# A streaming-encoder block whose front runs in five segments: the segments' sizes, when they run, and which engine adds which rows

## The reference, cut to what matters

```python
q = (h @ w_q).reshape(Bb, S, PEER_HEADS, 2, PEER_HALF)          # 8 heads, two halves of 128
scores = jnp.einsum('bshpd,pnd->bshpn', q, sub_keys)             # 128 keys for each half
vals, idx = lax.top_k(scores, 16)
cand = vals[..., 0, :, None] + vals[..., 1, None, :]             # 16 x 16 sums
top_vals, pos = lax.top_k(cand, 16)                              # 16 of 16384 experts
gates = softmax(top_vals)
u = jnp.take(u_tab, e, axis=0)                                   # 1024 numbers for each expert
act = gelu(jnp.einsum('td,thkd->thk', xt, u))
vv = jnp.take(v_tab, e, axis=0)
y = jnp.einsum('thk,thkd->td', g * act, vv)                      # added to x
```

## Time and profile before

| | us |
|---|---|
| median of 3 runs | 3558.37 (3557.22 to 3565.75) |
| the profiled execution, its own time | 3558.73 |
| its span, first to last instruction | 3556.9 |
| TensorE matmul busy | 2871.3 (81%) |
| VectorE busy | 2532.2 (71%) |
| ScalarE busy | 1419.6 (40%) |
| GpSimd busy | 1284.6 (36%) |
| moved by DMA | 1376.58 MB, mean 387 GB/s |

### The profile page before, as it was taken

How to read it: one execution, slowest core, us unless ns; L and a number is a source line. 1 busy time by engine, 2 the same in 40 slices (tenths; PEclk the granted TensorE clock), 3 DMA queues, 4 the chain that set the end, 5 groups by cost and what they waited for, 6 DMA issues and landing times.

```text
span 3556.9 us, 35414 instructions
## 1 busy us (share of the span) xinstructions
PE 2871.3 (81%) x11192; PEld 1930.2 (54%) x11192; DVE 2532.2 (71%) x5329; ACT 1419.6 (40%) x3606; POOL 1284.6 (36%) x1028
## 2 busy tenths in 40 slices
PE   8878978899878787686998889778878687686765
PEld 7767856776544455363665557454445355363323
DVE  0248877767888887699678876798566756677664
ACT  2333453324344443334344453434343443433522
POOL 0014332323454444344434433433334333344441
PEclk9989989999989899888999899889999899898987
DMA  6589988989999999999999999999999999999995
GB/s 237 172 320 421 377 315 327 365 331 384 421 422 415 404 421 421 420 392 404 422 421 420 405 383 412 416 413 395 422 421 421 421 410 421 420 417 412 421 421 218
DMA packets 195916, 1376.58 MB, mean 387 GB/s; under 512 B 22401, under 2 KB 24321, under 8 KB 32018
## 3 DMA queue, kind: packets, MB, share of 16 engines
q0 software_dynamic: 147456, 1073.81, 73.5%
q1 hardware_dynamic: 48274, 300.51, 21.4%
HBM read 1363.22 MB, written 11.01 MB: 386 GB/s over the span
## 4 chain that ended last, share of the span: by engine, by line
PE 34%; DMA 30%; DVE 18%; issue 9%; ACT 7%; POOL 2%; another core or an unknown queue 0%; DVEq 0%; POOLq 0%; ACTq 0%; SPq 0%
DMA uv<-in_uv,idx 29%; PE bank L588 13%; PE ysum L780 8%; PE bank L598 8%; DVE acc L1321 5%; DVE uv L1293 4%; POOL uv L545 2%; PE bank L657 2%; DVE lidx L1146 1%; DVE vals L1143 1%; ACT bufX L856 1%; DMA slab<-in_slabs 1%; DVE bufE L1140 1%; DVE bufX L1111 1%; ACT bufX L813 1%
## 5 line engine op out<-in xcount | busy, mean ns | idle before, releaser
L545 POOL DMA_INDIRECT uv<-in_uv,idx x1024 | 1284.4, 1254 | 2214.9 <-DVE acc L1321 1033.5
L1293 DVE SCALAR_TENSOR_TENSOR uv<-uv,hbuf 128x1024 f32<-128x1024 f32 x1024 | 1247.2, 1223 | 550.8 <-DMA uv<-in_uv,idx 526.4
L780 PE MATMUL ysum<-uv,diag 128*128 128x512 f32 x2152 | 1121.3, 665 | 418.7 <-ACT diag L1044 416.4
L780 PEld LDWEIGHTS ysum<-uv,diag 128*128 128x128 f32 x2152 | 433.6, 211 | 965.9 <-ACT diag L1044 514.1
L1321 DVE SCALAR_TENSOR_TENSOR acc<-uv,dots,acc 128x1024 f32<-128x1024 f32 x486 | 622.3, 1281 | 86.6 <-ACT dots L1035 69.9
L1030 ACT ACTIVATE dots<-dots 128x2 f32<-128x2 f32 x512 | 103.0, 201 | 1148.3 <-DVE uv L1293 1137.0
L588 PE MATMUL bank<-bufA,slab 128*128 128x256 f32 (+1 forms) x2400 | 439.3, 342 | 5.5 <-ACT bufB L813 5.4
L588 PEld LDWEIGHTS bank<-bufA,slab 128*128 128x128 f32 x2400 | 390.8, 194 | 74.1 <-issue 36.4
L598 PE MATMUL bank<-slab,bufA 128*128 128x256 f32 x1408 | 318.1, 385 | 4.9 <-ACT bufA L842 3.7
L598 PEld LDWEIGHTS bank<-slab,bufA 128*128 128x128 f32 x1408 | 271.3, 194 | 63.5 <-issue 20.8
L1035 ACT ACTIVATE dots<-dots,gexp 128x1 f32<-128x1 f32 x1024 | 245.9, 287 | 20.9 <-ACT dots L1030 0.4
(11 more groups left out here) (146 smaller groups left out, 2426.5 us busy)
## 6 DMA issues: line engine op xcount, KB each, us to landing
slab<-in_slabs SPq DMA_DIRECT2D x255, 1024.0 KB
uv<-in_uv,idx POOLq DMA_INDIRECT x1024
x_d<-acc SPq DMA_DIRECT2D x7, 512.0 KB, 8.1
bufA<-in_x SPq DMA_DIRECT2D x3, 1024.0 KB
bufA<-x_d SPq DMA_DIRECT2D x3, 1024.0 KB
out<-bufA SPq DMA_DIRECT2D x3, 1024.0 KB
bufE<-in_g_ffn SPq DMA_DIRECT2D x5, 512.0 KB, 9.0
bufX<-in_g_fin SPq DMA_DIRECT2D x5, 512.0 KB, 20.9
```

The source lines that it names most:

```text
L545: nc.gpsimd.indirect_dma_start(out=uv[:, at % NS, :], out_offset=None, in_=a["uv"], in_offset=bass.IndirectOffsetOnAxis(ap=idx[:, g % 4, k ...
L780: ins = mm(ysum[:, c, :], diag[:, m % DS, :], uv[:, at % NS, D + c * 512:D + c * 512 + 512], start=(m == first), stop=(m == last))
L1293: v.scalar_tensor_tensor(out=row, in0=row, scalar=1.0, in1=hbuf[:, i % HB, :], op0=ALU.mult, op1=ALU.mult, accum_out=dots[:, g % 3, k:k + ...
```

## The change

The segments become 1, 1, 2, 2 and 2 tiles, so `AT` goes from (0, 1, 3, 5, 7) to (0, 1, 2, 4, 6) and `MOVED` from tiles 2, 4, 6 to 3, 5, 7. The second segment, now one tile, is due in step 28 instead of 50, and the closing of segment 0 with its opening puts two stages in a step. The due steps of the other segments follow from the same rule as before: 114, 242 and 370. Only groups 0 and 1 have their tails in a segment now (3 and 4); the tail of tiles 4 and 5 stands by itself, from step 405. The lists of a tile go by the tile's number modulo 3 instead of its place in the segment. Tiles 0 and 1 give 5 of a head's 16 rows to TensorE (`SOME`), tiles 2 to 5 `ODD`, tiles 6 and 7 `MOST`, from a tile's row 6 on.

```diff
@@ -1,3 +1,4 @@
+import math
 from contextlib import ExitStack
 
 import numpy as np
@@ -30,7 +31,7 @@
 LOW = -3.0e38
 
 
-SEGS = (1, 2, 2, 2, 1)
+SEGS = (1, 1, 2, 2, 2)
 NSEG = len(SEGS)
 TT = max(SEGS)
 SEG = TT * P
@@ -45,6 +46,8 @@
 
 NS = 10
 HB = 2
+
+LS = 3
 STEPS = TOPK // 2
 ROWS = NHEAD * TOPK
 END = NHEAD * STEPS
@@ -56,11 +59,12 @@
 
 
 ODD = tuple(range(1, TOPK, 2))
+SOME = tuple(range(1, TOPK, 3))
 MOST = tuple(k for k in range(TOPK) if k % 4)
-ON_PE = [MOST, ODD, ODD, ODD, ODD, MOST, MOST, MOST]
-
-SPARE = [100] + [6] * (NTILE - 1)
-IS_PE = [at % TOPK in ON_PE[at // (NH * TOPK)] and at % (NH * TOPK) >= SPARE[at // (NH * TOPK)] and at < ROWS - 4
+ON_PE = [SOME, SOME, ODD, ODD, ODD, ODD, MOST, MOST]
+
+SPARE = 6
+IS_PE = [at % TOPK in ON_PE[at // (NH * TOPK)] and at % (NH * TOPK) >= SPARE and at < ROWS - 4
          for at in range(ROWS)]
 
 PE_UPTO, DVE_UPTO = [0], [0]
@@ -71,7 +75,7 @@
 
 
 GROUPS = ((0, 1), (2, 3), (4, 5), (6,), (7,))
-HOST = {0: 2, 1: 3, 2: 4}
+HOST = {0: 3, 1: 4}
 GUEST = {h: q for q, h in HOST.items()}
 TAIL = ["T0", "T1", "pg0", "pg1", "pg2", "pg3", "pp", "mx", "T2"]
 LAST_GROUP = len(GROUPS) - 1
@@ -129,6 +133,11 @@
 BEHIND.update({f"lg{b + 1}": f"va{b}" for b in range(2 * TT - 1)})
 
 
+
+
+DUE = [AT_ONCE - 2, PER_TILE // 2 - 4] + [PER_TILE * AT[s] - AHEAD - 2 for s in range(2, NSEG)]
+
+
 def plan():
 
     found = []
@@ -142,14 +151,14 @@
         names = front_names(s)
         if not s or s - 1 in GUEST:
             names = OPENING + names
-        due = PER_TILE * AT[s] - AHEAD - 2 if s else AT_ONCE - 2
+        due = DUE[s]
         last = len(names) - 1
         begin = found[-1][0] + 1 if found else due - last
         for i, n in enumerate(names):
             stand(s, n, begin + i * (due - begin) // last)
-        more, gap = closing(s), 2 if s in GUEST else 1
-        for i, (of, n) in enumerate(more):
-            stand(of, n, due + gap * (i + 1))
+        pace = 2 if s in GUEST else 1 if s else 0.5
+        for i, (of, n) in enumerate(closing(s)):
+            stand(of, n, due + math.ceil(pace * (i + 1)))
     for q, tiles in enumerate(GROUPS):
         if q == LAST_GROUP:
 
@@ -339,8 +348,8 @@
         acc = sb("acc", [P, 2, D])
         x2 = [acc[:, (NTILE - 1) % 2:(NTILE - 1) % 2 + 1, :] if q == LAST_GROUP else x1 for q in range(len(GROUPS))]
         diag = sb("diag", [P, DS, P])
-        vals = sb("vals", [P, TT, NH, 2, TOPK])
-        lidx = sb("lidx", [P, TT, NH, 2, TOPK], U32)
+        vals = sb("vals", [P, LS, NH, 2, TOPK])
+        lidx = sb("lidx", [P, LS, NH, 2, TOPK], U32)
         lidf = sb("lidf", [P, 2, TOPK])
         tv = sb("tv", [P, TOPK])
         negmax = sb("negmax", [P, 1])
@@ -1132,7 +1141,8 @@
                 lists = []
                 for t in range(SEGS[s]):
                     for half in range(2):
-                        lists.append((vals[:, t, h, half, :], lidx[:, t, h, half, :],
+                        slot = (AT[s] + t) % LS
+                        lists.append((vals[:, slot, h, half, :], lidx[:, slot, h, half, :],
                                       ysc[:, h % 2, t, half * NK:half * NK + NK]))
                 for c in (slice(0, 8), slice(8, 16)):
                     if c.start:
@@ -1220,7 +1230,7 @@
 
                 base = TK * m
                 i, h = divmod(m, NH)
-                slot = i - AT[seg_of(i)]
+                slot = i % LS
                 val = vals[:, slot, h]
                 if base + j:
                     dve.wait_ge(topk_step, base + j)
```

## The result

The changed kernel takes 3535.55 us (median of 6 runs, 3530.7 to 3545.11) against 3559.94 for the kernel before (6 runs): ratio 0.993, 95% interval 0.9914 to 0.9946, that is 24 us or 0.7% faster.

The account below looks back on a forecast made before the run. DMA bytes at 421.5 GB/s were taken as the bound: 3266 us, plus starved time (DMA engines short of work) of 113 at start-up, 111 in the steps and 43 at the end, gave 3533 of span, so 3534; range 3498 to 3575.

Parts of the forecast that it names:

- three demands of about equal size: Steps 15 to 50 before: DMA 260 us, PE 267, DVE 242, taking turns and stretching each other to 320.
- C: Steps 50 to 114, segment 2's two-tile front: DMA 400 us, PE 356, DVE 350; 22 us starved.
- The transfers of patterns: Steps 136 to 242 repeat 72 to 178 of before, 13 us starved; 242 to 370 repeat 178 to 306, 26.
- A: Steps -7 to 28, two stages in a step beside rows: 28 us starved, with bounds of 8 and 65.
- the ring: Gather slots, 10 rows holding 25 us; expected to cover the lone tail of tiles 4 and 5, steps 405 to 421.
- 417 GB/s or more: Sign: from step 370 the windows read at least this rate until the last 80 us.
- The milestones: Signs: step 50 at about 690 us, step 306 at some 2300, in front only from about step 430.
- Behind at both: Sign: later than the kernel before at step 50 (690 against 666.3 us) and step 306 (2300 against 2268.7).
- The crowd did not dissolve: Rival, 13%: the evener work up to step 136 starves little, 63 us in all over the plan's steps; 3485 us.
- only passed on: Rival, 20%: steps -7 to 28 and 50 to 114 starve 78 us, not 50; 3562 us, no change.
- lockstep: Rival, 12%: in steps 5 to 27 chained stages wait behind row work, 12.4 us a step; 3617 us, half covered 3575.
- The clock rival: Rival, 5%: PE's low clock makes late steps without stages take 6.5 us against 4.98, costing 90 us; 3624 us.

Follow-up runs that it names:

- e1: Changed kernel with the second segment due in step 50 again and one stage a step in the first closing: 3567.2 us, ratio to before 1.0016.
- e2: Changed kernel with the old split of the rows between TensorE and VectorE: 3567.2 us, ratio to before 1.0011.
- e4: Changed kernel with the stages of the lone tails three steps apart instead of two: 3527.2 us, ratio to before 0.9904.
- e5: Changed kernel loading only half the columns of each weight piece after the first three: 3433.5 us, ratio to before 0.9645.
- e6: Kernel before, loading only half the columns of each weight piece after the first three: 3435.9 us, ratio 0.9648.
- e3: Kernel before with the new split of the rows alone: 3578.9 us, ratio 1.0054.
- e8: Changed kernel with the second segment due in step 36 instead of 28: 3536.1 us, ratio to before 0.993.
- e9: e4 with segment 2's closing, with segment 3's opening, at 1.75 steps a stage instead of 1: 3522.6 us, ratio to before 0.9895.
- e10: e9 with segment 4's closing and the tail inside it at 2.5 steps a stage instead of 2: 3519.8 us, ratio to before 0.9888.

## Why the prediction was right

The forecast was 3534 us with 3515 to 3549 for the likeliest case; measured are 3535.6, and a span of 3533.1 against 3533 in the sum.

*The bound.* The account, bytes at a ceiling of 421.5 GB/s plus starved time, gave the right sum. But it can't be tested by the total: with the same bytes, a difference in span is a difference in starved time by definition. What the runs test is where it arises, and there the placing of the crowds is shown: taking back the run-ahead brings 59 us into steps 72 to 114 (e1), the old split 32 into 306 to 370 (e2), and the tail's pace works on steps 405 to 421 (e4). e5 and e6 add how thin the bound is, and correct the picture that I had of steps 15 to 50: of "three demands of about equal size" that stretch each other, the weight bytes are none, for half of them can go and the stretch stays at 320 us (e6). Nor do VectorE's late additions set it (e3).

*The terms.* C was right in each part: 168.6 MB forecast, 426.2 x 0.397 = 169.2 moved; PE 356 and 353.8 us; DVE 350 and 351.0; starved 22 and 24.8. Steps 114 to 136: PE 149 and 147.4, starved 15 and 13.1. The transfers of patterns held: 136 to 242 has 9.7 (13) and 242 to 370 has 31.6 (26; the same stages starve 23 to 28 in e1, e4, e8, e9 and e10), in the places in which steps 72 to 306 had them. Steps 114 to 370 took 1602.8 us, and steps 50 to 306 of before 1602.4.

*Two terms failed, in opposite directions.* A was priced at 28 us for want of a row with two stages in a step, and took 14.4 (16 to 21 in later runs with the same plan there): DMA share 1.01 up to step 15 with PE at 84%. The last term, 4 us for steps 370 to 504, took 16.2. I had written that the ring covers the lone tail of tiles 4 and 5; it covers its load, but not two-tile stages at two steps with 12 of 16 rows on PE (8.2 us; 1.5 at three steps in e4, 4.4 in e9). The closing with the tail of tiles 2 and 3 took 7.5, and had room to 2.2 (e10). I had compared both with steps 434 to 504 of before, whose segment was one tile wide. So "417 GB/s or more" from 370 on failed too: the windows read 407 and 389 up to step 421. That the total is right to 2 us is luck, these two errors cancelling.

*The milestones.* Step 50 came at 652 us, not 690, and step 306 at 2277, not 2300. The sum doesn't use them. 690 needs step -7 at about 222 us; the 157 MB moved up to step 28 less A's 118 leave 39 for the time before, and with 113 us of starving they put it at 205. "Behind at both" was wrong for step 50, where the kernel is in front (652 against 666.3 us); at step 306 it is behind (2268.7 before), at 434 still (3072.1 against 3063.2), and in front by step 504 (3453.4 against 3476.6).

*The rivals.* The crowd did not dissolve (C starved). It was not only passed on: A and C starved 39 us, not 78. (By the plan it is 23 more slabs up to step 114, not 18; the sum doesn't use it.) Something like lockstep is real but local: 371.3 to 501.0 is 10.0 us a step, under the 10.4 at which it would have decided. Its place is narrow. Of the 14.4 us, 12.7 lie in steps 14 to 20:

```profile
363.90:386.10 22.20, 13.54 (x59) 7.88 (x60) 10.88 (x24) 11.53 (x33) 1.80 (x2) 0.77 0.86 354
386.10:404.90 18.80, 12.63 (x89) 10.65 (x88) 17.18 (x32) 13.36 (x36) 8.39 (x7) 0.90 0.98 382
404.90:424.90 20.00, 18.58 (x104) 12.69 (x103) 9.02 (x14) 8.43 (x18) 3.56 (x3) 0.84 0.66 265
```

In e1 and e8 the same work stood in steps 30 to 38 and 18 to 26 and starved 11.7 and 11.6 us. The timeline of steps 17 to 20 shows how (start, length, engine, idle time before it and its cause):

```profile
404.27 1.97 PE L660 MATMUL bank<-ident,bufX 128*128 128x128 f32 x8 [6.17 <-DVEq L1227]
...
406.92 3.68 PE L666 MATMUL bank<-bufX,sv 128*64 128x512 f32 x4 [0.69 <-ACT bufX L822]
...
410.63 0.59 ACT L822 ACTIVATE bufQ<-bank 64x512 f32<-64x512 f32 x1 [3.77 <-PE bank L666]
...
420.38 0.94 POOL L554 DMA_INDIRECT uv<-in_uv,idx  x1 [18.12 <-PE ysum L789]
...
422.46 1.28 DVE L1331 SCALAR_TENSOR_TENSOR acc<-uv,dots,acc 128x1024 f32<-128x1024 f32 x1 [10.25 <-ACT dots L1044]
```

The value stage goes to and fro between PE and ScalarE over two banks; PE first waited 6.17 us for VectorE. Behind it stands PE's row, so a gather was 18.1 us late for its slot, and VectorE's addition waited 10.25 us for ScalarE's weights. That this exchange is the cause is read from the trace and from three placings; it is not shown, as no run took it away. A rival stands untested: in these windows PE mostly isn't waiting. It is busy 18.6 of the 20.0 us in which most starves (404.9 to 424.9), and 91 to 96% of the four starved windows in e1 and e8. Plain PE work, more in these few steps than the rows leave room for, would show the same. Only in the two windows before, with PE at 61 and 67%, does PE wait much. The clock rival: steps 421 to 452 ran at 0.84 and 421 GB/s, 158.6 / 31 = 5.1 us a step; with 421 GB/s reached, the lower clock cost nothing there.

## What to carry to other kernels

Where a transfer ceiling holds for most of the run, count bytes once and then sum the time that each stretch leaves the DMA engines short; that sum, stretch by stretch, says what a new order of the work is worth. It doesn't say what fewer bytes are worth: half the weight bytes gave back a third of their time. Judge the parts of such a change together: the sizes and the rows' split lost 5 and 17 us alone and won 24 as a pair. And when a stage type moves beside a wider segment, price it by a row of that width, for the two terms that were priced by a narrower neighbour or by no row at all were the ones that missed.

## What was not expected of the hardware

With 132 MB less to move, the changed kernel gave back a third of the time that these bytes take at the ceiling (102 of 313 us), and the crowded stretch of steps 114 to 136 took 165.3 us with all its weight bytes and 166.0 with half. A stretch can thus show 388 GB/s, 92% of the ceiling, and not get shorter when its weight bytes are halved (it moved 388 and then 345 GB/s).
